# Block compression by five products for four outputs, with the projection's norms and gates moved among its units

## The chip, the cores and the metric

The kernel runs on one core of a Trainium2 chip. The metric is the device time of one execution in microseconds. TensorE's clock, as the profile shows it, is either full (1.00, 2.4 GHz) or half (0.50, 1.2 GHz).

## The reference, cut to what matters

The program is one inference step of a two-layer decoder: a sparse-attention layer, then a state-space layer, each followed by a gated feed-forward block, all in float32, for a prompt of 512 tokens and 8 samples of 4 new tokens (544 columns). The change touches the start of layer 0: the input projection with its head norms and gates, and the compression of the cached key and value rows into block rows.

```
proj = h @ w_in                      # q, three k/v pairs, 48 gates per token
q    = rms_norm(q);  kvs.k, kvw.k = rms_norm(...)   # per head of 64
gate = sigmoid(gate)

# compress_blocks: rows (B, T, 4 groups, 64), blocks of 32, stride 16
chunks = rows.reshape(b, n_chunk, 16, 4, 64)
for m in range(2):
    part = einsum("bcjgd,jdh->bcgh", chunks + pe[m], w1[m])   # 1024 -> 256
    pre  = pre + part[:, m:m + n_blk]
out = silu(pre) @ w2                 # 256 -> 64
kc  = rms_norm(compress_blocks(k)),  vc = compress_blocks(v)
```

So the hidden value of block n is chunk n times w1[0] plus chunk n+1 times w1[1]. Each of 8 samples has 2048 cached rows (16 pages of 128), 128 chunks and 127 blocks; the prompt adds 32 chunks.

## The kernel before, in words

All engines run their own instruction lists, and semaphores order them. `InOrder` (`dve_do`, `act_do`, `pool_do`) makes an engine wait for each operation before its next. `meet` lines up the four compute engines at the end of a phase. SP issues most loads, GpSimd (POOL) some.

**Phase 1** (`p1_*`) projects in 10 units of two 128-feature tiles, each by seven half-size products (`product`, L339). ScalarE copies two of the seven (`copy_product`), VectorE adds the others up (`sum_products`, L365 to L378) and multiplies each tile by rstd (L611); GpSimd forms weight sums (`weight_sums`, L385 to L392) two units ahead. The tiles come in the order q, kc, vc, ks, kw, vs, vw. After all units, TensorE sums the squares by head (L529), multiplies for the gates (L543), spreads the reciprocal roots over each head's rows (L553) for 12 tiles through two pairs of PSUM banks, and gathers gates by row (L561). VectorE takes a reciprocal (L616), scales the tiles (L623 to L630), forms the sigmoids (L634, L635). Then all meet.

**Phase 2** (`p2_*`) compresses in 16 units, one per sequence and kind (key or value), in pairs of sequences. The sequence with the prompt's chunks added has 320 columns instead of 256. SP loads a unit's 16 pages into one of two row buffers; a load waits until the unit two before has made its first products (L711), after SP has loaded sixteen page numbers. A unit works by odd and even block positions and, per half of the 256 hidden features, makes **three products** of eight matmuls each for two outputs: (w1[0] + w1[1]) times the odd chunks, shared (L788), w1[1] times the next even chunk less the odd one (L794), w1[0] times the even less the odd chunk (L800). VectorE forms the two differences (L914 and L915, L921) and adds the products (L945, L953); ScalarE copies the shared product with the bias (L873) and applies Silu (L862, L865). The second layer (`second`, L760 keys, L763 values) of a unit runs inside the next unit. VectorE adds the weights once (L905), TensorE makes the bias from the position vector with the vector as the stationary operand (L735, L742), and GpSimd copies the prompt's chunks in eight small transfers (L996) after VectorE has turned them (L935). After the last unit come the key norm's squares on ScalarE (L882), its sums (L814), a root, a reciprocal and the spreads (L825, L832), then another meeting.

**Phase 3** (`p3_*`) turns the value tiles (L1159, L1164) and then computes the compressed scores (L1179), the first use of the compressed keys.

What orders the work around the change is written out by hand: the place of each call in an engine's list, `claim` for the PSUM banks (a product waits for the last reader of its bank), and one semaphore per kind of step.

Of the kernel before, what the change touches and what calls it, by code (L numbers as in the profile page):

```python
# [15 lines left out]
ALU = mybir.AluOpType  # L16
# [3 lines left out]
P = 128  # L20
# [162 lines left out]
def build(nc, t):  # L183
    ctx = ExitStack()
    with ctx:
# [108 lines left out]

        unit_at, at = {}, 0
# [64 lines left out]
        def sum_products(dve, do, u, regs, c0, c1, after_u=None):  # L360

            p1, p4, v, uu = regs
            dve.wait_ge(f_mm, multiplied(u, 1))
            dve.wait_ge(f_copied, 2 * u + 1)
            do(dve.tensor_tensor(c0[:, n1], p1, bank_in(u, 1), ALU.add), f_added)  # L365
            dve.wait_ge(f_mm, multiplied(u, 3))
            do(dve.tensor_tensor(v, p1, bank_in(u, 3), ALU.add), f_added)  # L367
            dve.wait_ge(f_mm, multiplied(u, 4))
            do(dve.tensor_tensor(uu, v, bank_in(u, 4), ALU.add), f_added)  # L369
            if after_u:  # L370
                after_u()
            dve.wait_ge(f_mm, multiplied(u, 5))
# [46 lines left out]
        class Norm:  # L419
# [34 lines left out]
            def pe(self, pe):  # L454
                for h in range(2):
                    claim(pe, 2 * self.q + h, n_rt, self.roots + 1)
                for kt in range(KT):
                    pe.wait_ge(n_sq, self.tiles + kt + 1)
                    for h in range(2):
# [20 lines left out]
                     q=norm_banks(U_NSA_IN))  # L480
# [3 lines left out]
        g_mm, g_col, g_neg, g_exp, g_rows, g_done = [sem(f"gate_{n}") for n in  # L484
                                                     ("product", "col", "neg", "exp", "rows", "done")]
        NORMED = [("q", kt) for kt in range(KT)] + [("ks", 0), ("ks", 1), ("kw", 0), ("kw", 1)]
        TILE_DST = [("q", kt) for kt in range(KT)] + [(n, i) for n in ("kc", "vc", "ks", "vs", "kw", "vw")
                                                      for i in range(2)]
# [20 lines left out]
        def p1_pe(pe):  # L509
            pe.wait_ge(ca_in, 16)  # L510
            b11, _, b21, b22 = four_blocks(hT)
            for u in range(10):
# [11 lines left out]

            pe.wait_ge(in_ev, 20)
            for j in range(12):
                pe.wait_ge(hs_sq, j + 1)
                for h in range(2):
                    last = pe.matmul(ps[0:24, h, 0:HALF], window[:, 34 - 2 * j:58 - 2 * j],  # L529
                                     nsq[:, j, h * HALF:(h + 1) * HALF], start=j == 0, stop=j == 11)  # L530
            last.then_inc(hs_ss, 1)

            pe.wait_ge(n_r, 1)
            pe.wait_ge(par_in, 16)
            for i in range(5):
                o, n = i * P, P if i < QT else NS
                last = pe.matmul(ps[0:n, 2, i:i + 1], rstd[0:1, o:o + n], ones[0:1, 0:1], start=True, stop=True)
            last.then_inc(g_col, 1)
            wg = par[:, PAR["w_gate"]].rearrange("p (k c) -> p k c", k=KT)
            for i in range(5):  # L540
                o, n = i * P, P if i < QT else NS
                for kt in range(KT):
                    last = pe.matmul(ps[0:n, 3, i * 48:(i + 1) * 48], hT[:, kt, o:o + n], wg[:, kt],  # L543
                                     start=kt == 0, stop=kt == KT - 1)
            last.then_inc(g_mm, 1)

            pe.wait_ge(hs_r, 1)
            for j in range(12):
                if j >= 2:
                    pe.wait_ge(hs_out, j - 1)  # L550
# [2521 lines left out]
```

## Time and profile before

| | us |
|---|---|
| median of 3 runs | 2516.94 (2515.99 to 2520.11) |
| profiled execution, its own time | 2514.76 |
| its span | 2512.8 |
| TensorE busy | 2300.0 (92%) |
| VectorE busy | 1280.1 (51%) |
| GpSimd busy | 786.6 (31%) |
| ScalarE busy | 514.7 (20%) |
| last product of the projection ends | 152.8 |
| first product of phase 2 starts | 219.0 |
| last product of phase 2 ends | 589.6 |
| compressed scores start | 616.7 |

The profile is of one execution. A busy share says how long an engine worked, not whether anything waited for it; so the table's last four lines, taken from the timeline, mark the stretches that the change touches. Recorded times of a matmul overlap the next; the distance between two groups' starts is what a group costs. A float32 matmul has two records.

### The profile page before, as it was taken

The page shows a single profiled execution, that of the slowest core. Times are in us where ns is not written, and L with a number is a line of the kernel's source. Part 1 is how long each engine was busy: PE and PEld are TensorE (multiplying, and loading weights), DVE is VectorE, ACT ScalarE, POOL GpSimd, SP SyncE. Part 2 cuts the span into 40 slices and gives each one's busy share as a digit, 9 for nine tenths or more (in the row PEclk, how much of TensorE's full clock was granted, in tenths as well). Part 3 has the DMA queues.
Part 4 walks back from the last instruction along what each step waited for, and adds up shares of the span by engine and source line. Part 5 has one row for each costly group of instructions (what it writes and reads, how often), then busy time and mean ns, then how long its engine had stood idle before and what let it go on. Part 6 is the DMA issues. An engine that isn't in the chain of part 4 may idle for free.

```text
span 2512.8 us, 34405 instructions
## 1 busy us (share of the span) xinstructions
PE 2300.0 (92%) x12318; PEld 1822.5 (73%) x12318; DVE 1280.1 (51%) x2109; ACT 514.7 (20%) x1205; POOL 786.6 (31%) x660
## 2 busy tenths in 40 slices
PE   7998999997788767999998999999778999999899
PEld 6876888876556545888886878787444778888687
DVE  5436332332577413555664238876785545566522
ACT  2111111112555521211110013232444011111000
POOL 4301000001100264433334415554464333334342
PEclk9987999998689878999999999999878899999999
DMA  4224223321200498212111222222231111221112
GB/s 158 83 84 129 87 87 97 101 76 52 96 9 1 151 312 324 111 67 95 74 68 58 93 90 76 76 85 73 101 123 79 67 68 67 86 83 69 63 75 82
DMA packets 87450, 237.15 MB, mean 94 GB/s; under 512 B 11281, under 2 KB 60562, under 8 KB 72946
## 3 DMA queue, kind: packets, MB, share of 16 engines
q1 hardware_dynamic: 80258, 205.07, 23.1%
q0 software_dynamic: 7024, 29.90, 3.5%
q8 instruction: 99, 1.62, 0.3%
q14 instruction: 69, 0.57, 0.1%
HBM read 218.46 MB, written 23.73 MB: 96 GB/s over the span
## 4 chain that ended last, share of the span: by engine, by line
PE 57%; DVE 8%; issue 3%; ACT 2%; POOL 2%; DMA 2%; POOLq 1%; DVEq 0%; ACTq 0%; SPq 0%
PE ps L339 47%; PE ps L1204 1%; DMA sbuf<-w_nsa_out 1%; PE ps L1248 1%; ACT sbuf L1309 1%; PE ps L460 1%; PE ps L1228 1%; ACT sbuf L1317 1%; DVE sbuf L2171 1%; POOL sbuf L2788 1%; PE ps L1179 1%; POOLq L1497 1%; PE ps L2413 1%; DVE sbuf L2681 1%; PE ps L2361 1%
## 5 line engine op out<-in xcount | busy, mean ns | idle before, releaser
L339 PE MATMUL ps<-sbuf 128*128 128x272 f32 x6048 | 1409.9, 396 | 51.4 <-DVE sbuf L1929 19.4
L339 PEld LDWEIGHTS ps<-sbuf 128*128 128x128 f32 x6048 | 1158.3, 192 | 301.5 <-DVE sbuf L1929 20.3
L385 POOL TENSOR_TENSOR sbuf<-sbuf 128x512 f32<-128x512 f32 (+2 forms) x90 | 137.3, 1525 | 716.8 <-PE ps L339 599.6
L358 ACT ACTIVATE sbuf<-ps 128x272 f32<-128x272 f32 x180 | 71.6, 398 | 1110.9 <-PE ps L339 1081.8
L367 DVE TENSOR_TENSOR sbuf<-sbuf,ps 128x272 f32<-128x272 f32 x90 | 39.4, 437 | 248.3 <-PE ps L339 247.4
L392 POOL TENSOR_TENSOR sbuf<-sbuf 128x512 f32<-128x512 f32 (+2 forms) x90 | 145.7, 1619 | 7.8 <-PE ps L339 1.0
L389 POOL TENSOR_TENSOR sbuf<-sbuf 128x512 f32<-128x512 f32 (+2 forms) x90 | 140.1, 1557 | 7.1
L386 POOL TENSOR_TENSOR sbuf<-sbuf 128x512 f32<-128x512 f32 (+2 forms) x90 | 138.4, 1537 | 7.1
L788 PE MATMUL ps<-sbuf 128*128 128x256 f32 (+1 forms) x512 | 122.5, 391 | 3.6 <-DVE sbuf L905 3.6
L800 PE MATMUL ps<-sbuf 128*128 128x256 f32 (+1 forms) x512 | 120.0, 385 | 0.0
L794 PE MATMUL ps<-sbuf 128*128 128x256 f32 (+1 forms) x512 | 120.0, 385 | 0.0
L788 PEld LDWEIGHTS ps<-sbuf 128*128 128x128 f32 x512 | 96.4, 191 | 22.8 <-issue 5.5
L794 PEld LDWEIGHTS ps<-sbuf 128*128 128x128 f32 x512 | 96.2, 188 | 18.6
L800 PEld LDWEIGHTS ps<-sbuf 128*128 128x128 f32 x512 | 96.0, 188 | 18.6
L945 DVE TENSOR_TENSOR sbuf<-sbuf,ps 128x256 f32<-128x256 f32 (+1 forms) x32 | 13.8, 430 | 181.9 <-PE ps L794 181.9
L373 DVE TENSOR_TENSOR sbuf<-sbuf,ps 128x272 f32<-128x272 f32 x90 | 39.4, 437 | 130.7 <-PE ps L339 130.1
L376 DVE TENSOR_TENSOR sbuf<-sbuf 128x272 f32<-128x272 f32 x90 | 103.4, 1149 | 3.1
L369 DVE TENSOR_TENSOR sbuf<-sbuf,ps 128x272 f32<-128x272 f32 x90 | 39.4, 437 | 125.8 <-PE ps L339 125.0
L996 POOL DMA_DIRECT2D sbuf<-sbuf x16 | 9.8, 620 | 291.1 <-PE ps L788 274.7
L1924 DVE TENSOR_TENSOR sbuf<-sbuf 128x544 f32<-128x544 f32 x88 | 92.9, 1056 | 3.0
L365 DVE TENSOR_TENSOR sbuf<-sbuf,ps 128x272 f32<-128x272 f32 x90 | 39.4, 438 | 83.5 <-PE ps L339 67.7
L1391 DVE CUSTOM_DVE_ANT_0 sbuf<-ps,sbuf 128x128 f32<-128x128 f32 (+3 forms) x128 | 57.0, 490 | 38.4 <-PE ps L1204 24.2
(348 smaller groups left out, 2525.8 us busy)
## 6 DMA issues: line engine op xcount, KB each, us to landing
sbuf<-w_gu SPq DMA_DIRECT2D x44, 1024.0 KB, 6.3
sbuf<-cmp_pages SPq DMA_DIRECT2D x256, 128.0 KB, 2.3
sbuf<-w_down SPq DMA_DIRECT2D x32, 704.0 KB, 5.2
sbuf<-w_ssd_in SPq DMA_DIRECT2D x20, 1024.0 KB, 4.8
sbuf<-w_nsa_in SPq DMA_DIRECT2D x10, 1024.0 KB, 4.8
sbuf<-sel_k SPq DMA_DIRECT2D x64, 128.0 KB, 4.0
sbuf<-sel_k POOLq DMA_DIRECT2D x64, 128.0 KB, 4.3
sbuf<-sel_v SPq DMA_DIRECT2D x64, 128.0 KB, 3.8
```

The source lines that it names most:

```text
L339: last = pe.matmul(ps[:, bank_of(u, j), 0:HALF], a[:, kt * P:(kt + 1) * P], b[:, kt], start=kt == 0, stop=kt == kts - 1)
L358: do(act.activation(dst, bank_in(u, j), ACT.Copy), f_copied)
L376: do(dve.tensor_tensor(c1[:, n1], c1[:, n1], p4, ALU.add))
L385: do(pool.tensor_tensor(sv[:, 0], a21, a22, ALU.add), f_sums)
L386: do(pool.tensor_tensor(sv[:, 1], sv[:, 0], a11, ALU.subtract), f_sums)
L389: do(pool.tensor_tensor(sv[:, 2], a11, a21, ALU.subtract), f_sums)
L392: do(pool.tensor_tensor(sv[:, 3], a12, sv[:, 1], ALU.subtract), f_sums)
L788: last = pe.matmul(shared, ws[:, kt, hs], rows[:, kt, :, :, 1], start=kt == 0, stop=kt == KT - 1)
L794: last = pe.matmul(odd, w1(kv, 1, kt)[:, hs], e[:, kt], start=kt == 0, stop=kt == KT - 1)
L800: last = pe.matmul(even, w1(kv, 0, kt)[:, hs], d[:, kt], start=kt == 0, stop=kt == KT - 1)
L1391: dve.tensor_tensor_reduce(S_ring[:, n % S_BUFS, 0:w], ps[:, x, 0:w], cn_("dist")[:, SEQ - w:SEQ], -float(slope[head_of(gp * 4 + r, x % 2) ...
L1924: do(dve.tensor_tensor(c[:, x], c[:, x], rstd, ALU.mult), g_took if v % 2 == 0 else None)
```

## The change

- The projection's tile order becomes q, ks, kw, kc, vc, vs, vw, and its PSUM banks are six, `(7u + j) % 6`; banks 6 and 7 hold norms and gates. Gate products run before unit 2, the exponentials and sigmoids in unit 3, the gates by row before unit 4, head sums inside unit 7 before its third product, the twelve spreads before the first six products of units 8 and 9, one bank pair for all. VectorE's scalings go between its steps of `sum_products`. GpSimd loads rows for the first new unit after its sums of unit 6. Both meetings go (phase 1 and phase 2).
- Phase 2 has 8 units: a kind and a **pair of sequences** each, all keys, then all values; the prompt's chunks are in the fourth pair of each kind (288 columns, the others 256).
- A unit makes **five products for four outputs**, per half of the hidden features: ten products of eight matmuls, in the order MID, FIRST, LAST, SUM, DIFF for half 0, then the same for half 1. VectorE's `transform` writes five moving operands T_all (one copy), each as soon as the product of the unit before has read it in half 1; the rows (two buffers, one per sequence of the pair) are last read by DIFF, which then releases the next load: first sequence by SP, second by GpSimd. The rows' order within a page is now r (four chunks) by c (two), so four sources lie in runs of two.
- Of a half's five products ScalarE copies MID and SUM, VectorE takes FIRST and LAST (one operation each) and makes the four outputs with six operations (`four_outputs`). ScalarE applies Silu with the bias in place, the whole half at once.
- GpSimd makes the weights for MID, SUM and DIFF: two adds, one add, one subtraction of 2048 elements, once for keys and again at unit 4 for values, from w1 in ring slots 2 and 3, which are loaded again for values.
- The bias is now made with the weights stationary: 32 matmuls of one column per kind. ScalarE turns the prompt's rows (32 copies).
- Key squares, sums, root, reciprocal and spreads move into unit 4.

```diff
         def bank_of(u, j):
+            if u < U_NSA_OUT:
+                return (7 * u + j) % 6
...
+                if u == 2:
+                    gate_products()
+                if u == 4:
+                    gates_by_row()
...
+                    if u == NORM_UNIT and j == 2:
+                        head_sums()
+                    if u >= SPREAD_UNIT and j < 6:
+                        spread(6 * (u - SPREAD_UNIT) + j)
...
+            def between(u):
+                def at_step(step):
...
+                    if u == NORM_UNIT and step == 1:
+                        dve.wait_ge(hs_rt, 1)
+                        do(dve.reciprocal(rq[0:24], rq[0:24]), hs_r)
+                    if u >= SPREAD_UNIT:
+                        for j in {0: (0, 1), 1: (2, 3), 2: (4,), 3: (5,)}[step]:
+                            normed(6 * (u - SPREAD_UNIT) + j)
...
+                if u == NORM_UNIT:
+                    transform(dve, do, 0, 0)
...
         def p2_sp(sp):
...
+            for u in range(1, NU):
+                sp.wait_ge(rows_read[0], u)
+                load_rows(sp, u, 0)
+                if u == PAIRS:
+                    for i, j in enumerate((T_FIRST, T_LAST)):
+                        sp.wait_ge(c_mm, product_at(u - 1, j, 1) + 1)
+                        sp.dma_start(w_raw[i], t["w1"][2 + i]).then_inc(w_in[(s0 + 2 + i) % RING], 16)
...
+            for u in range(NU):
+                for ht in range(2):
+                    for j in range(5):
+                        products(u, j, ht)
+                        if (ht, j) == (0, T_MID) and u >= 1:
+                            if u == PAIRS + 1:
+                                prompt_spread()
+                            second(pe, u - 1)
+                        if (ht, j) == (0, T_LAST) and u == 0:
+                            bias_product(0)
...
+        def transform(dve, do, u, j):
...
+            if u >= 1:
+                dve.wait_ge(c_mm, product_at(u - 1, j, 1) + 1)
...
+                if j == T_MID:
+                    do(dve.tensor_tensor(dst, d[:, 3], d[:, 1], ALU.subtract), c_t if part else None)
+                elif j == T_FIRST:
+                    do(dve.tensor_tensor(dst, d[:, 0], d[:, 2], ALU.subtract))
+                elif j == T_LAST:
+                    do(dve.tensor_tensor(dst[:, :, :, 0], d[:, 0, :, :, 1], d[:, 2, :, :, 0], ALU.subtract))
+                    do(dve.tensor_tensor(dst[:, :, 0:n - 1, 1], d[:, 0, :, 1:n, 0], d[:, 2, :, 0:n - 1, 1], ALU.subtract))
+                    do(dve.tensor_copy(dst[:, :, n - 1, 1], d[:, 2, :, n - 1, 1]))
+                elif j == T_SUM:
+                    do(dve.tensor_tensor(dst, d[:, 1], d[:, 2], ALU.add))
+                else:
+                    do(dve.tensor_tensor(dst, d[:, 1], d[:, 2], ALU.subtract), read)
+            if j == T_FIRST:
+                do(dve.scalar_tensor_tensor(out, mid, 0.5, out, ALU.mult, ALU.add), c_t)
+            elif j == T_LAST:
+                do(dve.scalar_tensor_tensor(out, mid, -2.0, out, ALU.mult, ALU.add), c_t)
+            elif j == T_SUM:
+                do(dve.tensor_tensor(out, out, mid, ALU.subtract), c_t)
+            elif j == T_DIFF:
+                do(dve.scalar_tensor_tensor(out, out, 3.0, mid, ALU.mult, ALU.add), c_t)
...
+            def four_outputs(u, ht):
...
+                do(dve.scalar_tensor_tensor(y[:, 2], mm, 1.0 / 6, m1, ALU.mult, ALU.add))
+                do(dve.scalar_tensor_tensor(y[:, 1], mm, -1.0 / 6, m1, ALU.mult, ALU.add), c_dve)
+                do(dve.tensor_tensor(y[:, 0], y[:, 0], y[:, 2], ALU.add))
+                do(dve.tensor_tensor(y[:, 3], y[:, 3], y[:, 1], ALU.add))
+                do(dve.scalar_tensor_tensor(y[:, 2], m2, 2.0 / 3, y[:, 2], ALU.mult, ALU.add))
+                do(dve.scalar_tensor_tensor(y[:, 1], m2, 1.0 / 3, y[:, 1], ALU.mult, ALU.add), c_pre)
...
+            for u in range(NU):
+                if u == 0:
+                    for j in (T_FIRST, T_LAST, T_SUM, T_DIFF):
+                        transform(dve, do, 0, j)
+                else:
+                    transform(dve, do, u, T_DIFF)
...
+                take_outer(u, T_FIRST, 0)
+                take_outer(u, T_LAST, 0)
+                four_outputs(u, 0)
                 if u + 1 < NU:
...
+                    transform(dve, do, u + 1, T_MID)
+                take_outer(u, T_FIRST, 1)
...
+                    transform(dve, do, u + 1, T_FIRST)
+                take_outer(u, T_LAST, 1)
...
+                    transform(dve, do, u + 1, T_LAST)
+                four_outputs(u, 1)
...
+                    transform(dve, do, u + 1, T_SUM)
...
+            raw_there(pool, 0)
+            pool.wait_ge(f_mm, multiplied(8, 6))
+            sum_mid()
+            pool.wait_ge(f_mm, multiplied(9, 6))
+            sum_sum()
+            pool.wait_ge(in_ev, 20)
+            pool.wait_ge(hs_out, 12)
+            pool.dma_start(t["out_kv"], kvT).then_inc(stored, 16)
+            load_rows(pool, 1, 1)
+            prompt_rows(0)
+            pool.wait_ge(c_turn, 32)
+            pool.wait_ge(stored, 16)
+            sum_diff()
+            for u in range(2, NU):
+                pool.wait_ge(rows_read[1], u)
+                load_rows(pool, u, 1)
+                if u == PAIRS:
+                    prompt_rows(1)
+                    raw_there(pool, 1)
+                    for j, do_sum in ((T_MID, sum_mid), (T_SUM, sum_sum), (T_DIFF, sum_diff)):
+                        pool.wait_ge(c_mm, product_at(u - 1, j, 1) + 1)
+                        do_sum()
```

## Rows read from the trace of the kernel before

**Rows 1.** Chain that ended last, of the whole page, shares of the span by engine
```profile
PE 57%; DVE 8%; issue 3%; ACT 2%; POOL 2%; DMA 2%; POOLq 1%; DVEq 0%; ACTq 0%; SPq 0%
```

**Rows 2.** Timeline of TensorE about the gap: start us, us, engine, line, operation, records
```profile
149.68 3.14 PE L339 MATMUL ps<-sbuf 128*128 128x272 f32 x13
219.04 5.39 PE L788 MATMUL ps<-sbuf 128*128 128x256 f32 x16 [3.59 <-DVE sbuf L905]
```

**Rows 3.** Timeline of TensorE (and L882) from the last unit product to the scores
```profile
585.99 3.64 PE L800 MATMUL ps<-sbuf 128*128 128x256 f32 x16
593.24 1.90 ACT L882 ACTIVATE sbuf<-sbuf 128x2032 f32<-128x2032 f32 x1
595.47 5.33 PE L814 MATMUL ps<-sbuf 128*32 128x127 f32 x32 [2.75 <-ACT sbuf L883]
604.44 5.78 PE L825 MATMUL ps<-sbuf 32*64 32x127 f32 x64 [3.52 <-DVE sbuf L962]
616.74 5.04 PE L1179 MATMUL ps<-sbuf 64*128 64x31 f32 x32 [0.73 <-ACT sbuf L1290]
```

**Rows 4.** Groups by line, first 330 us: busy us, mean ns, idle before
```profile
L529 PE MATMUL ps<-sbuf 128*24 128x272 f32 x48 | 12.9, 433 | 2.1 <-DVE sbuf L611 2.1
L543 PE MATMUL ps<-sbuf 128*128 128x48 f32 (+1 forms) x80 | 12.2, 335 | 0.0
L553 PE MATMUL ps<-sbuf 24*64 24x272 f32 x96 | 22.0, 657 | 0.0
```

**Rows 5.** Windows: start:end, length, busy us (records) of PE, PEld, DVE, ACT, POOL, PEclk, DMA share, GB/s
```profile
196.00:198.00 2.00, 2.00 (x12) 0.96 (x10) 1.40 (x4) 0.00 (x0) 0.00 (x0) 0.50 0.00 0
664.00:668.00 4.00, 2.98 (x30) 1.99 (x28) 2.23 (x13) 2.75 (x13) 0.00 (x0) 1.00 0.00 0
```

**Rows 6.** Timeline of TensorE inside the units
```profile
227.76 0.95 PE L742 MATMUL ps<-sbuf 128*128 128x1 f32 x8
302.44 3.64 PE L794 MATMUL ps<-sbuf 128*128 128x256 f32 x16
305.93 3.64 PE L800 MATMUL ps<-sbuf 128*128 128x256 f32 x16
319.84 1.88 PE L763 MATMUL ps<-sbuf 128*127 128x64 f32 x16
342.56 1.14 PE L760 MATMUL ps<-sbuf 128*64 128x127 f32 x16
547.12 4.49 PE L800 MATMUL ps<-sbuf 128*128 128x320 f32 x16
```

**Rows 7.** Groups of VectorE by line and form, from 215 to 610
```profile
L921 DVE TENSOR_TENSOR sbuf<-sbuf 128x2048 f32<-128x2048 f32 x14 | 32.1, 2294 | 0.5
L914 DVE TENSOR_TENSOR sbuf<-sbuf 128x1536 f32<-128x1536 f32 x14 | 26.7, 1908 | 0.5
L915 DVE TENSOR_TENSOR sbuf<-sbuf 128x480 f32<-128x480 f32 x14 | 14.9, 1062 | 0.0
L945 DVE TENSOR_TENSOR sbuf<-sbuf,ps 128x256 f32<-128x256 f32 x28 | 11.8, 422 | 154.4 <-PE ps L794 154.4
```

**Rows 8.** GpSimd issues page loads; then the landing of L716's (SP) and L1500's (both queues)
```profile
622.14 9.34 POOL L1500 DMA_DIRECT2D sbuf<-sel_k  x16 [5.54 <-issue]
636.70 9.32 POOL L1500 DMA_DIRECT2D sbuf<-sel_v  x16 [5.22 <-issue]
...
DMA to landing us min/median/max: 1.9/2.3/5.9
DMA to landing us min/median/max: 2.0/4.3/8.3
```

**Rows 9.** Two-source operations of VectorE and GpSimd beside each other, and of GpSimd alone
```profile
17.70 2.24 DVE L397 TENSOR_TENSOR sbuf<-sbuf 128x1088 f32<-128x1088 f32 x1
18.87 2.20 POOL L392 TENSOR_TENSOR sbuf<-sbuf 128x512 f32<-128x512 f32 x1
...
L1701 POOL TENSOR_TENSOR sbuf<-sbuf 128x2048 f32<-128x2048 f32 x4 | 14.5, 3622 | 8.7 <-DMA sbuf<-const_n 8.6
```

More of the change, by code:

```diff
@@ L572, in p1_act @@
             norm1.square(act, do)
-            for u in range(11):
-                if u < 10:
-                    copy_product(act, do, u, 0, in_regs[0])
+            for u in range(10):
+                copy_product(act, do, u, 0, in_regs[0])
                 if u == 0:
@@ new lines, in seq_at, with load_rows @@
+        def seq_at(u, part):
+            return 0 if part == 0 else 4 * (groups_of(u) - 2 * NPAGE)
+        def load_rows(eng, u, part):
+            kv, b = u // PAIRS, 2 * (u % PAIRS) + part
+            dst = (rows_a[:, 0:NPAGE * 256] if part == 0 else rows_0b if u == 0 else rows_b).rearrange(
+                "p (i n) -> p i n", n=256)
+            _, numbers = nc.values_load_multi_w_load_instructions(
+                pages[0:1, b * NPAGE:(b + 1) * NPAGE], engines=[eng.engine], min_val=0, max_val=NPHYS - 1)
+            for i, page in enumerate(numbers):
+                eng.dma_start(dst[:, i:i + 1], t["cmp_pages"][bass.ds(page, 1), kv].rearrange("o p n -> p o n")
+                              ).then_inc(rows_in[part], 16)
@@ L706, in p2_sp, with raw_there, second @@
+        SP.append(p2_sp)
+        def raw_there(eng, kv):
+            for i in range(2):
+                in_slot(eng, slot_at["w1"] + 2 * kv + i)
+        w2 = par[:, PAR["w2"]].rearrange("p (v h n) -> p v h n", v=2, h=2)
+        def second(pe, u):
+            kv, q = kind_of(u)
+            pe.wait_ge(c_hid, 2 * (u + 1))
+            hid = [by_positions(u, ht) for ht in range(2)]
+            if kv == 0:
                 if u == 0:
-                    sp.wait_ge(n_ss, 1)
-                elif u == 1:
-                    sp.wait_ge(met, 4)
-                else:
-                    sp.wait_ge(c_shared, 2 * (u - 1))
@@ L804, in p2_pe @@
-            pe.wait_ge(c_mm, 2 * NU)
+                            last = pe.matmul(ps[0:NC, 7, part * 256 + g * HD:part * 256 + (g + 1) * HD],
+                                             hid[ht][:, g, at:at + NC], w2[:, 1, ht], start=ht == 0, stop=ht == 1)
+                if with_prompt(u):
+                    for g in range(GROUPS):
+                        for ht in range(2):
+                            last = pe.matmul(ps[0:NCP, 6, g * HD:(g + 1) * HD], hid[ht][:, g, CHUNKS:CHUNKS + NCP],
+                                             w2[:, 1, ht], start=ht == 0, stop=ht == 1)
@@ L805, in p2_pe @@
             for i in range(4):
                 pe.sem_inc(w_used, 1)
-            second(NU - 1)
-            for b in range(NB):
-                for gp in range(2):
-                    j = 2 * b + gp
-                    pe.wait_ge(hs_sq, len(NORMED) + 1)
-                    last = pe.matmul(ps[0:32, 0, 0:NC], window[:, 34 - 2 * j:66 - 2 * j], kc_sq[:, b, gp],
-                                     start=j == 0, stop=j == 15)
-            for gp in range(2):
-                last = pe.matmul(ps[0:4, 1, 0:NCP], window[:, 34 - 2 * gp:38 - 2 * gp], kc_sq_p[:, gp],
-                                 start=gp == 0, stop=gp == 1)
@@ L969, in p2_dve @@
[L969 to L982 removed]
+            gain = par[:, PAR["qk"]][:, 1:2]
@@ L1282, in p3_act @@
             do = act_do
-            for k in range(4):
-                act.wait_ge(a_vt, k + 1)
+            for n, k in enumerate(V_TURNS):
+                act.wait_ge(a_vt, n + 1)
                 br, gp = k // 2, k % 2
```

786 lines of the change are left out of this document (428 added, 358 removed).

## The prediction

> **What bounds the kernel now.** I read the page's chain first: TensorE has 57% of it, nearly all projection products outside this edit [rows 1], so the edit counts only by when TensorE reaches the first compressed scores. The timelines bound the stretch: the projection's last product ends at 149.7 + 3.1 = 152.8, the first unit product starts at 219.0 [rows 2], the last unit product ends at 589.6 and the scores start at 616.7 [rows 3]. So there are three pieces: a gap of 66.2, 370.6 of units in which TensorE is never idle for long, and a tail of 27.1. In the gap TensorE does 12.9 of head sums, 12.2 of gate products and 22.0 of spreading [rows 4], the last at the granted clock 0.50 [rows 5]; the rest is reciprocals, sigmoids, meeting and preparing.
>
> **The products.** Eight products of 256 columns take 3.64 us as recorded and follow each other every 3.49; with 320 columns 4.49 [rows 6]. Before: 14 x 6 x 3.49 + 2 x 6 x 4.34 = 345. After: 6 x 10 x 3.49 + 2 x 10 x 3.92 (288 columns, between) = 288. **57 us of TensorE work go.** The second layer stays alike: two sequences together 2 x 1.1 for keys, 2 x 1.9 for values [rows 6].
>
> **Projection.** All that comes between its products lies on TensorE's path. Gates: 12.2 [rows 4] and 1 for the small ones, then a restart at the low clock, 5.39 - 3.64 = 1.8 [rows 2, 6], from 0 to 3.6. Gates by row 1. Head sums 11 (12.9 with a part at half clock). Spreads 22.0 at half clock, so 11 to 22; I take 11, for TensorE 75% busy with small work kept clock 1.00 [rows 5]. There is now one bank pair, so each spread waits for the last scaling; in unit 8 the first scaling (1.3 for its three parts) stands behind a 0.4 addition, two multiplications by rstd (0.8 each) and the MID transform (2.7, slowed by GpSimd), so it ends at 6.6, where the second spread wanted 2.75: a wait of 4. In unit 9, without the transform, 0.5. The reciprocal, exponentials and sigmoids are covered by the unit's remaining products (1.84 each, half of 3.64); uncovered, the reciprocal would cost 3.5. Sum 42; the products now end at X = 195.
>
> **VectorE's new work.** A two-source operation of 2048 takes 2.29, of 1536 in runs of three 1.91, of 480 single elements 1.06 [rows 7]. So 1024 elements in runs of two cost 1.24 (full rate) to 2.1 (the singles' rate); I take 1.3, as runs of three lose only 8%. MID is two of these, 2.7; FIRST, SUM and DIFF add one of 2048: 5.0; LAST has four of 480 to 512 singles, two tiny ones and a 2048: 7.3. One of the six output operations costs 0.42 (256 from PSUM [rows 7]) to 0.65 (at the singles' rate); with mixed forms I take 3.4 for six, range 2.5 to 3.9. Per unit that is 25.0 for the five, 2 x 3.4 and four takes of 0.5 (one product plus MID's copy, near the 0.42): 34 of VectorE against 37 of TensorE, so neither has the slack to cover the other's waits.
>
> The Trainium skill ("SBUF — State Buffer", the DMA port swizzle section) says that accesses run at full rate when a 16-byte line is hit at least twice, and pay for each new line. The rows agree [rows 7] for runs of three and of one. By that rule runs of two are full rate and all output writes, a line apart, pay: six would take 3.9 and a round 0.5 more.
>
> **Rows set the round.** T_all has one copy, rows two for two halves, and DIFF is the last reader. From the end of LAST for a unit: six outputs 3.4, SUM 5.0, DIFF's reads 2.7; then GpSimd (and SP, a step earlier) loads sixteen page numbers (5.5 and 5.2 before the first issue), issues 16 transfers in 9.3 and they land 4.3 later [rows 8]. With 5.2 taken, the rows are there at 29.9. Then half a MID 1.4, take 0.5, FIRST 5.0, take 0.5, LAST 7.3: **44.6 per round**. TensorE's own need is 34.9 + 2.1 for keys; it waits idle for the six outputs and the Silu (1.2, from 2032 elements in 1.90 [rows 3]) ahead of the second layer, which is free, as the rows are later still; the cold start behind that wait I count only where TensorE sets the end. Before, a load had two units' time; that cover is gone. In a unit with prompt rows (or the load for one) a round is 46.9.
>
> **Unit 0.** After X: two rstd multiplications, then FIRST beside GpSimd's weight sum, ready at 10; LAST 17.3, SUM 22.3, DIFF 27.3. VectorE's 1088 took 2.24 and GpSimd's 512 2.20 side by side, against 2048 in 3.6 for GpSimd alone [rows 9], so both slow by about 1.7. The bias now loads 32 weights of 128 columns: four took 0.95 [rows 6], so 7.6 to 10 with the clock down; I take 10. GpSimd's queue (SUM's weights, output store, rows 9.3, eight prompt copies 4.9, DIFF's weights) ends at 31. TensorE: FIRST 14, LAST 21, bias 31, SUM and DIFF 40.6, second half 17.4: 58. LAST for unit 1 follows from DIFF's end: FIRST's product frees its operand 7.0 later, take 0.5, FIRST 5.0, take 0.5, LAST 7.3, so X + 61.
>
> **Unit 4.** The value weights can load only after unit 3's LAST product, 7.8 before its end; 5 later GpSimd starts two adds of 3.6 [rows 9], slowed by VectorE: MID waits 7 (range 5 to 12, by neither or both running beside VectorE). On SP these loads stand behind the rows of unit 4, issued long before. Then products 34.9, second layer 2.6, bias 9, key sums 4 and spreads 4.6 (5.3 and 5.8 now, partly half clock [rows 3]), cold starts 3.5: 65.5. The key norm thus leaves the tail.
>
> **Sum.** LAST for unit 3: X + 61 + 44.6 + 46.9 = X + 152.5. Unit 4 starts 3.8 + 1.2 + 2.1 + 15.7 + 19.6 + 2 = 44.3 later, X + 197; unit 5 at X + 262. Unit 5's LAST 1, rounds 46.1 (two key scalings) and 46.9, then 3.8 + 1.2 + 3.7 + 35.3 + 2 = 46: X + 402 = 597. The tail is outputs 3.9, Silu 1.2, second layer 4.8, start 0.5 = 10.4, with the value transposes hidden beneath. Scores at 607.6, 9 earlier. The profiled execution took 2514.76, so 2505.7; the runs' median is 2.2 higher: **2508**. Of 57 + 16 us (products, tail) and the gap's 24, the rounds, unit 0 and unit 4 take nearly all.
>
> **Rivals.** A measurement here tells 0.2%, 5 us, from no change.
> - *Forecast, 0.38*: the round is 44 to 47. Own range 2496 to 2520: faster 0.25, same 0.10, slower 0.03.
> - *TensorE keeps the round, 0.22*: the numbers come faster on SP and GpSimd with nothing in front, the strided reads are free. Then LAST ends 20.3 after DIFF's product (as in unit 0), where the unit ends at 17.4; the second layer waits 2.9 + 3.4 + 1.2 - 3.5 = 4, and the round is 41, or 38.5 with a cheap LAST: four rounds give 15 to 24, 2484 to 2493, take 2488. Against: each issue gap before row loads is about 5 [rows 8].
> - *Two streams share the DMA engines, 0.12*: 32 transfers of 128 KB in one burst; the landing already goes from 2.3 for one queue to 4.3 where two issued together [rows 8]. Two us more in each of four rounds: 2516; same 0.08, slower 0.04.
> - *Slower: the clock falls in units 8 and 9, 0.16*: spreads of 24 rows between the products stayed at 0.50 for their whole 22 us [rows 4, 5]. If a third of such work lowers the clock, the 11 of spreads and part of 26 of products double: 18 to 37 more, 2530. It decides once the granted clock there is under about 0.75. For it: a stretch TensorE filled completely stayed low. Against: products fill two thirds. The Trainium skill ("TensorE: Matmul & The Clock Gate", What's actually happening) says activity releases a throttled default; this alone does not say whether spreads count.
> - *Slower: VectorE is the bound, 0.12*: runs of two cost like singles, 0.85 more on each of eight operations, of which seven lie in the round: 6 x 4 rounds and 6 in units 0 and 4: 2538. It decides when a 1024 takes over 1.7.
>
> The sum of chances: faster 0.47, same 0.20, slower 0.33. The range 2483 to 2541 reaches to each rival and leaves out the ends of the first and last.
>
> **What would show it.** Right: projection ends near 195 with clock 1.00 in its last two units; a gap on TensorE before each second layer of 3 to 6; VectorE's MID waiting for rows; unit starts 44 to 47 apart; unit 4 some 65; scores near 608. Wrong: MID never waits (then TensorE's round), the 1024s over 1.7, clock 0.50 in the last projection units, or unit 0 beyond 65.

## The result: 2.2% slower, and the profile after

The changed kernel takes **2574.03 us** (2567.12 to 2581.91, 4 runs) beside 2517.41 of the kernel before: ratio 1.0225, 95% interval 1.0194 to 1.0255. The forecast was 2508, the range ended at 2541. The profiled execution took 2573.70.

First the page of the changed kernel: its busy times and, against [rows 1], the chain by engine.

```profile
PE 2288.7 (89%) x12134; PEld 1817.3 (71%) x12134; DVE 1449.4 (56%) x2229; ACT 511.6 (20%) x1184; POOL 892.7 (35%) x796
...
PE 55%; DVE 7%; issue 3%; ACT 3%; POOL 2%; DMA 2%; POOLq 1%; DVEq 0%; ACTq 0%; SPq 0%
```

TensorE's busy time fell by only 11, although the unit products' own busy time fell by 56 (L788, L794 and L800 had 362.5, L921 has 306.5), and the chain barely moved: nothing here names a culprit, so I go by milestones. Three pieces, before and after: from 152.8, where the projection ended before, to the first unit's product, 66.2 to 62.8; units, 370.6 to 448.3; tail, 27.1 to 12.7. The differences (-3.4, +77.7, -14.4) sum to 59.9, or within rounding the scores' shift from 616.74 to 676.56. Against the kernel before, all of the loss is inside the units. For comparison with [rows 4], TensorE's groups in the first 330 us (gates, head sums, spreads):

```profile
L561 PE MATMUL ps<-sbuf 24*64 24x272 f32 x96 | 15.6, 445 | 12.3 <-DVE sbuf L656 12.3
L533 PE MATMUL ps<-sbuf 128*128 128x48 f32 (+1 forms) x80 | 13.2, 351 | 0.0
L552 PE MATMUL ps<-sbuf 128*24 128x272 f32 x48 | 11.2, 392 | 0.0
```

The spreads fell from 22.0 to 15.6, but 12.3 of waiting for a scaling (L656) came with them. TensorE's timeline at the places that answer to [rows 2, 3, 6]:

```profile
157.08 1.14 PE L561 MATMUL ps<-sbuf 24*64 24x272 f32 x8
158.14 2.10 PE L342 MATMUL ps<-sbuf 128*128 128x272 f32 x8
164.00 2.08 PE L561 MATMUL ps<-sbuf 24*64 24x272 f32 x8 [3.76 <-DVE sbuf L656]
195.98 2.07 PE L561 MATMUL ps<-sbuf 24*64 24x272 f32 x8 [8.56 <-DVE sbuf L656]
215.57 2.77 PE L921 MATMUL ps<-sbuf 128*128 128x256 f32 x12
...
328.44 4.71 PE L828 MATMUL ps<-sbuf 128*64 128x128 f32 x32 [7.22 <-ACT sbuf L996]
424.39 6.24 PE L921 MATMUL ps<-sbuf 128*128 128x256 f32 x16 [7.06 <-POOL sbuf L1162]
444.18 1.97 PE L828 MATMUL ps<-sbuf 128*64 128x128 f32 x8 [13.55 <-ACT sbuf L996]
521.73 7.06 PE L843 MATMUL ps<-sbuf 128*127 128x64 f32 x32 [10.49 <-DVE sbuf L1120]
676.56 3.62 PE L1387 MATMUL ps<-sbuf 64*128 64x31 f32 x16
```

A second layer of keys (L828) takes 4.71 behind its wait, one of values (L843) 7.06; before, two sequences took 2.3 and 3.8 [rows 6]. Windows show why: near 1.00 while products follow each other, a low clock at each restart behind a wait (columns as in [rows 5]). The last three windows are the bias of unit 4, 32 matmuls of one column. They follow products without a wait, and TensorE is busy throughout, yet the granted clock goes from 1.00 to 0.50 there; a low clock is thus not only the price of a wait.

```profile
164.00:168.00 4.00, 4.00 (x13) 2.35 (x14) 1.21 (x3) 0.00 (x0) 0.00 (x0) 0.50 0.00 0
200.00:215.00 15.00, 15.00 (x75) 9.69 (x74) 5.36 (x10) 0.40 (x1) 0.00 (x0) 0.97 0.01 1
328.00:336.00 8.00, 7.56 (x44) 6.84 (x45) 7.83 (x6) 0.77 (x2) 0.00 (x0) 0.63 0.00 0
336.00:360.00 24.00, 24.00 (x112) 20.72 (x111) 11.56 (x15) 1.92 (x3) 8.60 (x16) 1.00 0.54 176
...
458.00:460.00 2.00, 2.00 (x20) 1.99 (x18) 0.60 (x1) 0.00 (x0) 1.80 (x4) 1.00 0.90 279
460.00:462.00 2.00, 2.00 (x13) 2.00 (x12) 0.00 (x0) 0.00 (x0) 1.54 (x4) 0.56 1.04 342
462.00:469.00 7.00, 7.00 (x34) 7.00 (x35) 0.00 (x0) 0.00 (x0) 3.63 (x7) 0.50 0.99 333
```

The rows that matter most are VectorE's while it forms LAST for unit 4, beside GpSimd's of the same time (against [rows 9]):

```profile
415.04 4.84 DVE L1055 TENSOR_TENSOR sbuf<-sbuf 128x512 f32<-128x512 f32 x1
419.92 5.18 DVE L1056 TENSOR_TENSOR sbuf<-sbuf 128x480 f32<-128x480 f32 x1
425.13 4.39 DVE L1057 COPY sbuf<-sbuf 128x32 f32<-128x32 f32 x1
429.56 5.39 DVE L1055 TENSOR_TENSOR sbuf<-sbuf 128x512 f32<-128x512 f32 x1
434.98 1.00 DVE L1056 TENSOR_TENSOR sbuf<-sbuf 128x480 f32<-128x480 f32 x1
```

```profile
414.47 4.50 POOL L1161 TENSOR_TENSOR sbuf<-sbuf 128x2048 f32<-128x2048 f32 x1 [10.16 <-issue]
419.05 5.19 POOL L1162 TENSOR_TENSOR sbuf<-sbuf 128x2048 f32<-128x2048 f32 x1
424.32 5.14 POOL L1165 TENSOR_TENSOR sbuf<-sbuf 128x2048 f32<-128x2048 f32 x1
429.55 4.50 POOL L1168 TENSOR_TENSOR sbuf<-sbuf 128x2048 f32<-128x2048 f32 x1
```

Read the ends: 419.88, 425.10, 429.52, 434.95 on VectorE; 418.97, 424.24, 429.46, 434.05 on GpSimd. Each VectorE operation that begins beside a GpSimd one ends within 1 us of it, whatever its own size; a copy of 32 elements takes 4.39, while the last 480 takes 1.00 as GpSimd is done. The two engines **take turns, a whole operation at a time**. LAST for unit 4 took 23.5 instead of the 7.3 of the forecast, and the Silu, the second layer and every later operand stood behind it.

An operation that VectorE had already begun does not keep its turn either. In unit 0:

```profile
241.11 7.87 DVE L1069 SCALAR_TENSOR_TENSOR sbuf<-sbuf 128x2048 f32<-128x2048 f32 x1
242.29 4.54 POOL L1168 TENSOR_TENSOR sbuf<-sbuf 128x2048 f32<-128x2048 f32 x1
```

VectorE's operation starts 1.2 ahead of GpSimd's and ends 2.15 behind its end, nearly its whole own time of 2.29. It took 7.87, where the two own times, 2.29 and 3.62, sum to 5.9; why it lost more than a turn stays open. Four of the experiments' profiles below (`scale_first`, `numbers`, `later`, `numbers_later`) repeat it, with 7.86 to 7.88.

VectorE's groups by form in the units, against [rows 7]: runs of two at full rate (1234 ns), strided outputs slow (616 to 634).

```profile
L1059 DVE TENSOR_TENSOR sbuf<-sbuf 128x1024 f32<-128x1024 f32 x14 | 17.3, 1234 | 0.5
L1085 DVE SCALAR_TENSOR_TENSOR sbuf<-sbuf,ps 128x256 f32<-128x256 f32 x24 | 14.8, 616 | 33.5 <-PE ps L921 33.1
L1051 DVE TENSOR_TENSOR sbuf<-sbuf 128x1024 f32<-128x1024 f32 x12 | 14.7, 1226 | 10.9 <-DMA sbuf<-cmp_pages 7.1 <-PE ps L921 3.4
L1098 DVE SCALAR_TENSOR_TENSOR sbuf<-sbuf 128x256 f32<-128x256 f32 x12 | 7.6, 634 | 0.4
```

### The profile page after: what moved, and what is told of

Same layout as the page of the kernel before. It is cut to its first block, busy times and chain, and to the rows that moved or that the text cites. A ratio compares the mean times of both kernels' runs of the same rounds, so it can differ in the third digit from the quotient of the medians.

```text
span 2572.3 us, 34092 instructions
## 1 busy us (share of the span) xinstructions
PE 2288.7 (89%) x12134; PEld 1817.3 (71%) x12134; DVE 1449.4 (56%) x2229; ACT 511.6 (20%) x1184; POOL 892.7 (35%) x796
## 4 chain that ended last, share of the span: by engine, by line
PE 55%; DVE 7%; issue 3%; ACT 3%; POOL 2%; DMA 2%; POOLq 1%; DVEq 0%; ACTq 0%; SPq 0%
PE ps L342 46%; DMA sbuf<-w_nsa_out 1%; PE ps L1412 1%; PE ps L1456 1%; POOL sbuf L3001 1%; ACT sbuf L1519 1%; PE ps L467 1%; PE ps L1436 1%; ACT sbuf L1527 1%; DVE sbuf L2384 1%; PE ps L1387 1%; POOLq L1710 1%; PE ps L2574 1%; DVE sbuf L2142 1%; DVE sbuf L2137 1%
## 5 line engine op out<-in xcount | busy, mean ns | idle before, releaser
L342 PEld LDWEIGHTS ps<-sbuf 128*128 128x128 f32 x6048 | 1160.6, 192 | 309.4 <-issue 24.8
L921 PE MATMUL ps<-sbuf 128*128 128x256 f32 (+1 forms) x1280 | 306.5, 400 | 15.5 <-issue 8.5
L921 PEld LDWEIGHTS ps<-sbuf 128*128 128x128 f32 x1280 | 250.5, 197 | 68.1 <-issue 18.0
L372 DVE TENSOR_TENSOR sbuf<-sbuf,ps 128x272 f32<-128x272 f32 x90 | 39.4, 437 | 238.8 <-PE ps L342 237.8
L781 POOL DMA_DIRECT2D sbuf<-cmp_pages x128 | 69.1, 540 | 270.5 <-issue 264.7
L380 DVE TENSOR_TENSOR sbuf<-sbuf,ps 128x272 f32<-128x272 f32 x90 | 39.4, 438 | 128.1 <-PE ps L342 127.4
L375 DVE TENSOR_TENSOR sbuf<-sbuf,ps 128x272 f32<-128x272 f32 x90 | 39.4, 438 | 123.3 <-PE ps L342 122.4
L369 DVE TENSOR_TENSOR sbuf<-sbuf,ps 128x272 f32<-128x272 f32 x90 | 39.4, 437 | 105.2 <-PE ps L342 89.5
L1601 DVE CUSTOM_DVE_ANT_0 sbuf<-ps,sbuf 128x128 f32<-128x128 f32 (+3 forms) x128 | 57.0, 490 | 34.1 <-PE ps L1412 23.5
L1519 ACT ACTIVATE sbuf<-sbuf 128x128 f32<-128x128 f32 (+3 forms) x128 | 70.8, 563 | 7.0 <-DVE sbuf L1601 7.0
L2384 DVE SCALAR_TENSOR_TENSOR sbuf<-sbuf 128x568 f32<-128x568 f32 x72 | 58.4, 811 | 19.3 <-ACT sbuf L2283 17.0
L1436 PE MATMUL ps<-sbuf 128*128 128x128 f32 x320 | 52.0, 291 | 12.8 <-ACT sbuf L1527 12.7
L385 DVE TENSOR_TENSOR sbuf<-sbuf,ps 128x272 f32<-128x272 f32 x90 | 39.4, 438 | 40.3 <-PE ps L342 38.0
```

The source lines that it names most:

```text
L342: last = pe.matmul(ps[:, bank_of(u, j), 0:HALF], a[:, kt * P:(kt + 1) * P], b[:, kt], start=kt == 0, stop=kt == kts - 1)
L921: last = pe.matmul(product_of(u, j, ht), w[:, kt * 256 + ht * P:kt * 256 + (ht + 1) * P], moving[:, kt], start=kt == 0, stop=kt == KT - 1)
L1436: last = pe.transpose(ps[:, 4 + x % 2, j * P:(j + 1) * P], S_ring[:, n % S_BUFS, j * P:(j + 1) * P], ident)
L1519: act.activation(S_, S_, ACT.Exp, scale=-1.0, bias=low[:, 0, s % 3, x:x + 1], accum_out=low[:, 1, s % 3, x:x + 1]).then_inc(a_exp, 1)
L2384: do(dve.scalar_tensor_tensor(acc[:, x], raw[:, x, k:k + CONV], conv_w[:, c, k:k + 1], acc[:, x], ALU.mult, ALU.add), r_conv if k == 3 els ...
```

## The experiments

All medians are of 4 to 10 runs; the kernel before, beside them on the same chips, had 2515.6 to 2516.7. "Round" is from one LAST operand's end to the next on VectorE, and "round 5" the one from LAST for unit 5 to LAST for unit 6. The ratios in brackets are to the kernel before, with their 95% interval. The time behind the start of the compressed scores, which no edit touches, is 1893 to 1903 in the profiles of the change and its variants, so a few us of any total are no gain of an edit.

**Is it turns, or a factor?** Two kernels. `pieces` cuts each of GpSimd's weight sums into four of 512 elements; `dve_sums` gives the sums to VectorE (three operations of 2.29 per kind instead of four on GpSimd).

```diff
+            def by_part(out, x, y, op, signal, parts=4):
+                for i in range(parts):
+                    c = slice(i * 2048 // parts, (i + 1) * 2048 // parts)
+                    pool_do(pool.tensor_tensor(out[:, c], x[:, c], y[:, c], op), signal if i == parts - 1 else None)
...
-                pool_do(pool.tensor_tensor(w_of[T_SUM], w_raw[0], w_raw[1], ALU.add), c_w)
+                by_part(w_of[T_SUM], w_raw[0], w_raw[1], ALU.add, c_w)
...
+            if j == T_MID:
+                do(dve.scalar_tensor_tensor(w_of[j], w_raw[1], 2.0, w_raw[0], ALU.mult, ALU.add), c_w)
```

> The changed kernel with each of GpSimd's weight operations of 2048 columns cut in four of 512. Theory (the engines take turns whole operations at a time, so a short VectorE operation waits for the rest of GpSimd's): the waits shrink with the piece. The two rstd multiplications in unit 9 take about 3 to 4 together, not 9.6; the second copy of the LAST operations before unit 4, 24 in all for the transform, takes 12 to 15; the whole is 10 to 20 shorter, 2554 to 2564. Rival (both run at a reduced rate while together): the total is set by the amount of work, nothing changes, 2570 to 2578, the transform before unit 4 still over 20.

> The changed kernel with the weights of MID, SUM and DIFF made by VectorE (one operation of 2.3 each) instead of GpSimd: for keys in unit 9 after the last scaling and before the SUM and DIFF transforms, for values before unit 3's LAST transform, after it before SUM, and before DIFF. Theory (GpSimd's sums block VectorE): unit 9's wait of 8.6 goes, unit 0 gets some 2 shorter, LAST before unit 4 goes from 24 to 7.2, the second layer in unit 4 starts some 13 after the unit's start instead of 27, the whole is 22 to 32 shorter: 2542 to 2552. Rival (the time in unit 4 is the late value weights and the key norm, not the sums): only unit 9 gains, 8 to 10, 2564.

Measured: `pieces` **2557.12** (ratio 1.0156, 1.0139 to 1.0173), `dve_sums` **2546.42** (1.0113, 1.0096 to 1.013). Both are inside their forecasts. The same sums in smaller pieces block less: the small operations of LAST for unit 4, VectorE in `pieces`, where GpSimd's pieces follow each other from 405.43 on:

```profile
407.09 0.68 DVE L1085 SCALAR_TENSOR_TENSOR sbuf<-sbuf,ps 128x288 f32<-128x288 f32 x1
407.81 1.29 DVE L1055 TENSOR_TENSOR sbuf<-sbuf 128x512 f32<-128x512 f32 x1
409.13 1.94 DVE L1056 TENSOR_TENSOR sbuf<-sbuf 128x480 f32<-128x480 f32 x1
411.11 1.16 DVE L1057 COPY sbuf<-sbuf 128x32 f32<-128x32 f32 x1
412.30 2.15 DVE L1055 TENSOR_TENSOR sbuf<-sbuf 128x512 f32<-128x512 f32 x1
```

LAST takes 13.2 there, and 7.1 in `dve_sums`. Once the turns are under way, each operation takes its own time (1.00, 0.20, 1.07) and 0.9 to 1.1 more, about one piece of GpSimd (0.91 by size). A factor of 1.7 would not have cared for the piece's size. Only operations that find all their sources in SBUF are held: L1085, with one source in PSUM, takes 0.68, no more than in `dve_sums` without any GpSimd sum (0.68). Without GpSimd sums the first unit's product starts at 205.5 instead of 215.6, and unit 4's round (LAST 3 to LAST 4) is 51.6 instead of 66.4: 10 and 15 of the 27.6 won. That is net of VectorE's own 2.29 for each sum.

**The key scaling of the prompt.** `scale_first` scales the prompt's keys right behind the others in unit 4; in the change that scaling stands behind two operands of unit 5 in VectorE's list, and TensorE's second layer waits for it.

```diff
                     key_scale(3)
+                    key_scale(PAIRS)
...
-                    if u == PAIRS + 1:
-                        key_scale(PAIRS)
```

> The changed kernel with one VectorE operation moved: the scaling of the prompt's compressed keys stands right behind the fourth key scaling instead of behind the SUM and DIFF transforms of unit 5. Theory: TensorE's idle 10.5 before the first second layer for values is the wait for exactly this operation (it must free the bank); moved, the second layer waits for the Silu alone and starts some 9 to 10 earlier, so the whole is 8 to 12 shorter, 2562 to 2566. Rival: the wait passes to the SUM and DIFF operands, which VectorE finishes no earlier; the second layer moves, the unit's end doesn't, 2570 to 2576.

Measured **2564.65** (1.0187, 1.017 to 1.0204), 9.4 less, as forecast. The two rounds around it fell from 67.6 and 58.7 to 63.9 and 49.8, by 3.6 and 8.9, 12.5 together; of the other four rounds three shrank by 0.2 to 1.4 and the last grew by 0.8.

**What sets the round: rows or TensorE?** `numbers` moves the loading of the sixteen page numbers ahead of the wait for the buffer, on SP and GpSimd; `later` runs the second layer behind the LAST product; `numbers_later` does both.

```diff
                 pages[0:1, b * NPAGE:(b + 1) * NPAGE], engines=[eng.engine], min_val=0, max_val=NPHYS - 1)
+            if after:
+                eng.wait_ge(*after)
...
-                        if (ht, j) == (0, T_MID) and u >= 1:
+                        if (ht, j) == (0, T_LAST) and u >= 1:
                             second(pe, u - 1)
```

> The sixteen page numbers are loaded ahead of the wait for the row buffer instead of behind it, on both queues. Theory (the rows set the round in the changed kernel, but TensorE is close behind): VectorE's waits of 3.1 to 4.0 for the page rows ahead of the odd-chunk difference vanish, then the round is TensorE's: 9.2 from the end of the LAST operand to the first product (outputs 3.9, Silu, second layer at half clock) + 35.1 of products = 44.3 instead of 46.4, and 46.9 instead of 48.9. Five rounds by 2: 10 less, 2562 to 2567. Rival (the page numbers lie beside other work): within 3 of the changed kernel's 2574. Rival (the rows alone set the round): the full 5.2 in each of five rounds, 2548.

> The second layer of the unit before runs behind the third product of half 0 (LAST) instead of behind the first (MID). Theory (rows set the round): TensorE's waits of 4.6 to 8.3 for the Silu and the restarts at half clock go, but the rounds stay 46.4 and 48.9, as VectorE then waits the same for the rows; only in unit 5, where the second layer waits 10.5 for the key scaling, some 7 are gained: 2565 to 2571. Rival (TensorE's idle time and its cold restarts set the round): 7 per round as well, six of them: 2574 - 42 = 2532.

> Both edits together. Theory (two cycles of nearly equal length, rows and TensorE, so that each edit alone shows little): the round is 11.2 to the last read, 9.3 + 4.3 + 0.6 to the rows landed and 15.8 for three operands, 41.2 instead of 46.4: five rounds by 5.2 and the 7 of unit 5: 2574 - 33 = 2541, from 2536 to 2546, less than the sum of the two single gains (10 + 7) would give: 2557. Rival (the edits add up): 2557.

Measured: `numbers` **2557.84** (1.0176, 1.0153 to 1.0199), `later` **2553.58** (1.015, 1.0126 to 1.0174), both **2533.84** (1.008, 1.0055 to 1.0105). The first two key rounds, 46.4 and 48.9 in the change, were 44.6 and 45.4; 48.2 and 47.8; and with both 41.2 and 44.0. So in the plain round (the first) one edit alone gives 1.8 and the other nothing, and the pair gives 5.2 as forecast. Over the whole kernel the edits are not worthless alone: their medians are 16.2 and 20.5 less than the change's, and the pair's 40.2, near the sum of 36.7. All three medians lie below what I had expected, by 4, 11 and 2. For `numbers` the rounds gave the 10 of the forecast; the rest is a projection that ended 2.6 earlier, which no edit had touched, and the time behind the scores. VectorE's wait shows the handover. In the change, then in `later` (TensorE no longer idles, so VectorE comes to the rows earlier and waits longer):

```profile
307.50 2.49 DVE L1051 TENSOR_TENSOR sbuf<-sbuf 128x1024 f32<-128x1024 f32 x2 [3.06 <-DMA sbuf<-cmp_pages]
```

```profile
307.02 2.48 DVE L1051 TENSOR_TENSOR sbuf<-sbuf 128x1024 f32<-128x1024 f32 x2 [10.81 <-DMA sbuf<-cmp_pages]
```

In `numbers` the wait is gone, and the same operation starts at 302.25, 28.0 behind the LAST operand's end instead of 30.6. My expectation of `later` left out the last unit, where LAST's end to the last product fell from 49.9 to 38.7, by 11.2, because no second layer waits for a Silu ahead of that unit's products.

**Was the projection part a gain?** `norms_only` is the kernel before with the projection part alone (banks, order of the tiles, gates, sums and spreads among the units), both meetings and the old units kept.

> This is the kernel before with only the first part of the change: tile order, six product banks, gates, head sums and spreads among the projection's units; compression and both meetings as before. In the changed kernel the first unit product starts at 215.6 against 219.0, with two waits of 3.8 and 8.6 in units 8 and 9 that stand behind the MID transform and behind GpSimd's sum of 2048. Theory: without these two the spreads cost little more than their own time, the projection ends near 200, the first product of the units starts at 208 to 212 (meeting and preparation take about 9), and the whole is 7 to 11 shorter than before: 2506 to 2511. Rival: the spreads and the gates cost the same wherever they stand (half clock, one bank pair), then the first unit product starts at 217 to 221 and the whole is within 5 of before.

Measured **2525.8** (1.0032, 1.0017 to 1.0047): a miss, 15 above the range. TensorE's timeline names the cause. SP's list loads the compression weights, which wait for ring slots of unit 9, ahead of the first rows; the gap had covered that.

```profile
199.34 3.94 PE L341 MATMUL ps<-sbuf 128*128 128x272 f32 x16
206.85 3.63 PE L775 MATMUL ps<-sbuf 128*1 128x256 f32 x64 [3.57 <-DMA sbuf<-w]
223.81 6.11 PE L828 MATMUL ps<-sbuf 128*128 128x256 f32 x16 [13.32 <-DMA sbuf<-cmp_pages]
```

```diff
-            load_slots(sp, "w1", t["w1"], 4)
             sp.wait_ge(pages_in, 16)
             for u in range(NU):
+                if u == 1:
+                    load_slots(sp, "w1", t["w1"], 4)
```

> The kernel before with the projection part alone, and SP loading the first unit's rows ahead of the compression weights instead of behind them. Theory (the norms among the projection's units do save time, and the variant without this edit lost it as its first unit's product waited 13.3 for page rows, until 223.8): the first product starts when VectorE has its weights, near 214, so 9 to 10 less than that variant's 2525.8: 2514 to 2519, no different from the kernel before. Rival (the spreads beside products cost as much as the gap saved): within 3 of 2526.

Measured **2511.8** (0.9985, 0.9972 to 0.9998), 2 below the range and just under the kernel before: the first unit's product stands at 211.74 instead of 219.04. `norms_only` also separates the projection's own cost: its units 8 and 9 go from 157.3 to 203.3, 46.0, against 58.5 in the change, which has the MID transform between them and GpSimd's sums beside them.

**All together.** The edit below is that of `all7`. `all4` joins `numbers`, `later`, `dve_sums` and `scale_first`. `all5` also takes unit 3's keys before the DIFF weights and operand of unit 4; `all6` also reads SUM and DIFF from one row buffer, then from the other, before either is combined; `all7` takes unit 3's keys before combining SUM too.

```diff
+                    for part in range(2):
+                        transform(dve, do, u + 1, T_SUM, 0, (part,))
+                        transform(dve, do, u + 1, T_DIFF, 0, (part,))
+                    if u + 1 == PAIRS:
+                        take_k(u)
+                    transform(dve, do, u + 1, T_SUM, 1)
```

> Both edits, VectorE forming the three weight sums instead of GpSimd, and the prompt keys scaled with the others in unit 4. Theory: 2574 - 33 - 27.6 (measured for the weight sums alone) - 5 (what is left of the scaling once the second layer comes later) = 2508, from 2502 to 2516, faster than the kernel before (2517). Rival (the waits cover each other and VectorE, now with 9 more of work per kind and no slack, binds): over 2520.

> The four edits together, and in unit 4 VectorE takes the keys of the last key unit ahead of the DIFF weights and operand, not behind them, so that the bias products need not wait for it. Theory (TensorE's wait of 9.9 ahead of the bias and the half clock behind it, 13.8 for 64 records against 9.6 in unit 0, are on the path): 8 to 12 less than the 2503.9 of the four edits, 2492 to 2496. Rival (VectorE's own 25 of operands in that unit set its end): within 3 of 2504.

> As the one before, and VectorE reads the row buffers for SUM and DIFF one buffer after the other before it combines either, so that SP's load starts 4.8 and GpSimd's 2.3 earlier. Theory (with the four edits the page rows still set the rounds: waits of 5.3 for them in front of the odd-chunk difference): 2.3 less in each of four to five rounds, 9 to 12 less than the kernel without it. Rival (VectorE or TensorE binds by then): less than 4.

> As the one with early reads, and VectorE takes the last keys ahead of combining SUM for unit 4, not behind it. Theory (early reads gained in the rounds, 39.2 to 40.4 instead of 41.2 to 44.2, but gave it back in unit 4, where the bias waited 5.3 again and then ran at half clock, 13.8): the wait goes and the bias takes about 10, 5 to 9 less than 2495.5, so 2487 to 2491. Rival (the clock is low there whatever came before it, and something else ends the unit): 2493 to 2496.

| | median (runs) | ratio to before | LAST to LAST, units 1 to 7 |
|---|---|---|---|
| change | 2574.03 (4) | 1.0225 | 46.4 48.9 66.4 67.6 58.7 49.2 |
| all4 | 2503.94 (9) | 0.9956 (0.9942 to 0.9969) | 41.8 44.2 46.7 69.7 44.9 44.0 |
| all5 | 2496.31 (4) | 0.9919 (0.9902 to 0.9936) | 41.2 44.2 46.6 60.6 46.5 42.5 |
| all6 | 2495.54 (4) | 0.9923 (0.9906 to 0.9939) | 39.2 40.4 47.0 65.2 44.9 40.4 |
| all7 | **2491.50** (5) | **0.99** (0.9883 to 0.9917) | 39.1 40.4 46.8 62.3 46.5 40.4 |

`all4` is inside its forecast. The single gains, 40.2 for the pair, 27.6 and 9.4, would have given 2496.8, so they add up but for 7; 4 of these the forecast had told, as part of the scaling's gain is covered once the second layer comes later. `all5` gained 7.6 where 8 to 12 had been forecast. `all6` was told to gain 9 to 12 and its median gained 1: four rounds lost 1.6 to 3.8 each, near the 2.3 forecast, but unit 4 gave 4.6 back, since the keys were again taken late (its profile has the scores 6.1 earlier than `all5`, 593.9 for 600.0, so the medians show less than the stretch). `all7` has a median 4 lower, where I had put 5 to 9, but its profile does not show where: the scores start at 593.89 in both, since the round that holds the edit fell by 2.9 while the next grew by 1.6 and the stretch from the last product to the scores by 2.1. So that gain is not shown. Its bias, TensorE's timeline:

```profile
401.06 13.81 PE L867 MATMUL ps<-sbuf 128*128 128x1 f32 x64 [2.95 <-DVE sbuf L1130]
```

The wait ahead fell from 5.31 to 2.95, but the bias still took 13.8, where the change's in unit 0 took 9.56. The clock was 0.50 from its start to its end. In the change it took 11.59 with no wait ahead and the clock fell 2 us after its start; in `dve_sums` 10.98 behind a wait of 1.12, in `all5` 12.42 behind 2.75. So the bias comes to half clock whatever stands ahead of it, and the wait is not all that made it slow. Why it is low from its start in `all7`, after so short a wait, stays open. The change's idea, with its waits taken out and its sums on VectorE, thus beats the kernel before by 1.0%.

## Why the prediction was wrong, point by point

- **Projection** ("Sum 42", X = 195): X was 215.6, 20.6 late. Unit 8 began at 157.1, 30.1 later than the 127.0 of before, where gates and head sums had been given 27: 3 late. Units 8 and 9 took 58.5 instead of 41.2. Of the 17.3, 10.0 are GpSimd's first two sums (`dve_sums` takes them away): two multiplications by rstd, 0.8 each in the sum, took 9.6 beside them, and 1.5 in `dve_sums`. The rest is a spread with its product at 3.1 instead of 2.75, twelve times, and a half-clock restart behind the wait of 3.76, which I had as 4.
- **Unit 0** ("58", LAST at X + 61): 58.3 and X + 61.3. Right in sum, and the bias at 9.6 for 10. One term was off without harm: DIFF's operand was ready at X + 33.4 instead of 27.3 (the 7.87 above), hidden behind the bias.
- **"Rows set the round: 44.6"**: 46.4, and 48.9 for 46.9. The mechanism held (waits of 3.1 to 4.0 for the rows, 4.6 to 8.3 for the Silu on TensorE), the size was 2 short; the outputs were one term, 3.9 to 4.0 for 3.4. "The cold start I count only where TensorE sets the end" was the weak clause: `numbers` showed TensorE's cycle, 44.6 with its idle time and half-clock second layer, right behind the rows' 46.4.
- **Unit 4** ("65.5"): 86.7 from the end of unit 3's products, at 417.3, to unit 5's first product, at 504.1: 21 late, and **the step that failed**. Outside unit 0, where FIRST was given some 3 for the sum beside it, VectorE's operations beside GpSimd's sums were priced at their own time: LAST at 7.3, and the multiplications by rstd at 0.8 each. What stood behind it was the wrong mechanism: "So both slow by about 1.7", read from [rows 9] as a ratio. By size the two lines do not even give one ratio: a 1088 alone would take 1.22 (2048 in 2.29, rows 7) and a 512 of GpSimd 0.91 (2048 in 3.62), so the factors are 1.8 and 2.4. Together they take 2.13, and both took 2.2: turns. MID's wait of 7 came out at 7.06; but I let the sums delay TensorE alone and never asked which VectorE operations would run beside them. LAST took 23.5, and TensorE waited 13.55 ahead of the second layer, for which the sum had nothing. The other 8 are low clock: MID 6.2 for 3.5, the second layer 6.8 for 2.6, the bias 11.5 for 9 and the two products behind it 9.3 for 7, less the 3.5 told for cold starts. Without GpSimd's sums (`dve_sums`) unit 4 takes 72.3 and the wait is 8.6.
- **Round 5** ("46.1, two key scalings"): 58.7, 12.6 late. A wait I did not see: the sum has no term for the scaling of the prompt's keys, which is 0.3 of work but stands behind 10 of operands. `scale_first` took 8.9 from this round and 3.6 from the one before; the rest of the 12.6 is not traced.
- **Value rounds and tail** ("46.9", "46", "10.4"): 49.2, 49.9, 12.7. The second layer of values took 7.1 at half clock for 3.7.
- Shares of the 69 by which the scores came late (676.6 for 607.6): projection 21, unit 4 21, round 5 13, all else 14. `dve_sums` bears out the sums' part in the first two (10.0 and 14.4 less there, 27.6 in the median), `scale_first` the third. If their gains add, both together bring the median to 2537, inside the range, but still 29 above the forecast: the failed step alone does not explain the miss.
- One reading of [rows 7] was off without effect: runs of three cost 11% more per element than full rate (1908 for 1536 against 2294 for 2048), not 8%.
- **The rivals.** Runs of two like singles: no, 1234 ns. The clock falling in units 8 and 9: no, 0.97 from 200 to 215, low only behind the waits. Sharing of the DMA engines: no, rows landed 4.2 after the last issue for 4.3 told. TensorE keeps the round: false in the change; in `numbers`, where VectorE no longer waits for rows, true, but with 44.6 and not the 41 told. The clock did fall under small work, but in the bias of unit 4 (1.00 to 0.50 with TensorE busy), not under the spreads. "Slower" had 0.33 in the summary, and the rivals' own parts give 0.35 (and "same" 0.18, not 0.20); none of them had the mechanism that came.
- **The Trainium skill** ("SBUF — State Buffer", the DMA port swizzle section): its rule that a 16-byte line must be hit twice for full rate, with the singles' price from [rows 7], gave 3.9 for the six strided outputs. The trace agrees with it better than with my 3.4: they took 3.9 to 4.0, and runs of two ran at full rate.

## What to carry to other kernels

When two engines' rows are read side by side, compare each with its own time alone, and ask whether they sum: a "factor" between pieces of like length may be turns, and then the longest operation on one side is the price of every small one on the other (here, of those with all sources in SBUF). Place every moved wait in its engine's list and add what stands ahead of it, not its own work. When two cycles are within a few per cent of each other, judge an edit together with its partner and by the round it should shorten: alone the two here changed the first round by -1.8 and +1.9, together by -5.2, while their totals, 16 and 20 less, came in good part from elsewhere.

## What was not expected of the hardware

- A VectorE copy of 32 elements took 4.39 beside a GpSimd operation of 2048 and 0.20 without it; a 512 took 4.84 to 5.39 against 1.07, and with GpSimd pieces of 512 it took 1.3 to 2.2. The GpSimd operation itself took 4.50 to 5.19, against 3.62 for the one of [rows 9]. A VectorE 2048 begun 1.2 ahead of GpSimd's took 7.87 instead of 2.29. With one source in PSUM, VectorE kept its own time (0.68).
- An operation of 256 elements that writes every fourth element took 0.62 to 0.63, with a source in PSUM as with all in SBUF, where 256 contiguous took 0.42 [rows 7].
- Behind waits of 4.6 to 8.3 the second layer of keys took 4.1 to 4.7, where it takes 2.6 without a wait in `all6`; and 32 one-column matmuls, with no wait ahead and TensorE busy throughout, saw the granted clock go from 1.00 to 0.50.
